# Attention masks on another engine: a select on GpSimd for a minimum on VectorE, and latent sums, root and norm issued one by one

## The reference

```
h    = rmsnorm(x) * (1 + sc1) + sh1            # sc1, sh1, ... from c @ w_ada
proj = h @ w_in                                # q_lat 384, kv_lat 256, k_rope 32, swa q 512, k 128, v 128
q    = rmsnorm(q_lat) @ w_qb                   # 8 heads, 64 + 32 with rope
k, v = rmsnorm(kv_lat) @ w_kvb
y_mla = causal softmax attention, 8 heads, over all keys up to the query
y_swa = sliding window of 128 with ALiBi and sinks: own block of 128 keys and the one before
x = x + g1 * concat(y_mla, y_swa) @ w_o
x = x + g2 * relu(rmsnorm(x)... @ w_up)^2 @ w_down
out = rmsnorm(x)
```

## Time and profile before

| | |
|---|---|
| median of three runs | 945.23 us (944.41 to 946.27) |
| profiled execution, its own time | 945.04 us |
| span of its slowest core | 943.4 us (all cores 939.6 to 943.4) |
| mean granted TensorE clock | 0.955 to 0.961 of full speed |
| busy: PE, ACT, DVE, POOL | 829.5, 507.5, 412.7, 172.0 us |

### The profile page before, as it was taken

The page is one execution under the profiler, slowest core; times in us unless marked ns, Lnnn a source line. Parts: engine busy times, 40 slices in busy tenths (PEclk is TensorE's granted clock), DMA queues, the critical chain, the costliest instruction groups (busy, mean ns, idle before and its releaser), DMA issues.

```text
span 943.4 us, 13041 instructions; the slowest of 8 cores (939.6 to 943.4 us)
## 1 busy us (share of the span) xinstructions
PE 829.5 (88%) x4263; PEld 376.0 (40%) x4263; DVE 412.7 (44%) x673; ACT 507.5 (54%) x750; POOL 172.0 (18%) x182
## 2 busy tenths in 40 slices
PE   1758759877988899997998999999999999999994
PEld 0324323433443344443443444444444444444441
DVE  2264778757564752447843122221112222111566
ACT  3056465667776788884886433234443223445543
POOL 6040211212112110345640000000000000003331
PEclk9969979989999899998999999999999999999997
DMA  8993322432320052207838005040143100000224
GB/s 187 167 155 101 101 46 57 101 79 46 56 46 1 1 134 46 90 1 217 141 49 130 1 1 90 11 79 1 22 67 59 32 1 1 1 1 1 90 90 179
DMA packets 13585, 63.11 MB, mean 67 GB/s; under 512 B 1728, under 2 KB 1984, under 8 KB 9808
## 3 DMA queue, kind: packets, MB, share of 16 engines
q0 software_dynamic: 8192, 36.02, 23.5%
q1 hardware_dynamic: 5328, 26.27, 8.2%
HBM read 89.90 MB, written 8.39 MB: 104 GB/s over the span
## 4 chain that ended last, share of the span: by engine, by line
PE 74%; DVE 9%; ACT 6%; DMA 5%; issue 4%; POOL 1%; DVEq 0%; ACTq 0%; SPq 0%; POOLq 0%
PE ps L508 65%; PE ps L1021 5%; PE ps L965 5%; DMA arena<-wada 4%; DVE arena L1009 2%; ACT arena L990 2%; DMA arena<-xt 1%; DVE arena L1055 1%; DVE arena L563 1%; DVE arena L1057 1%; ACT arena L512 1%; DVE arena L1328 1%; ACT arena L1278 1%; ACT arena L514 1%; ACT arena L554 0%
## 5 line engine op out<-in xcount | busy, mean ns | idle before, releaser
L508 PE MATMUL ps<-arena 128*128 128x512 bf16 (+3 forms) x3623 | 742.2, 351 | 89.7 <-DMA arena<-wada 25.2
L508 PEld LDWEIGHTS ps<-arena 128*128 128x128 bf16 x3623 | 319.3, 99 | 474.8 <-issue 146.6
L1310 DVE SCALAR_TENSOR_TENSOR arena<-ps,arena 128x512 f32<-128x512 f32 x128 | 95.8, 750 | 314.5 <-PE ps L508 314.5
L1297 ACT ACTIVATE arena<-ps 128x512 f32<-128x512 f32 x128 | 76.4, 597 | 210.3 <-PE ps L508 209.8
L990 ACT ACTIVATE arena<-ps 128x1024 bf16<-128x1024 f32 x158 | 158.8, 1020 | 53.4 <-PE ps L965 27.5
L659 POOL TENSOR_TENSOR arena<-arena 128x512 f32<-128x512 f32 (+2 forms) x49 | 64.0, 1307 | 188.1 <-ACT arena L1156 186.9
L1021 PE MATMUL ps<-arena 128*128 128x512 bf16 (+1 forms) x320 | 87.9, 357 | 9.3 <-DVE arena L1009 8.7
L965 PE MATMUL ps<-arena 128*128 128x512 bf16 (+1 forms) x320 | 88.0, 358 | 3.6 <-ACT arena L990 2.6
L1298 ACT ACTIVATE arena<-arena 128x512 bf16<-128x512 f32 x128 | 80.9, 632 | 12.2 <-ACT arena L1297 0.6
L1013 POOL TENSOR_TENSOR arena<-arena 128x512 bf16<-128x512 f32 x32 | 41.9, 1311 | 201.1 <-ACT arena L1012 109.3
L1156 ACT ACTIVATE arena<-arena 128x512 bf16<-128x512 f32 x56 | 35.4, 632 | 43.0 <-DVE arena L1310 35.6
(11 more groups left out here) (62 smaller groups left out, 360.9 us busy)
## 6 DMA issues: line engine op xcount, KB each, us to landing
arena<-wada POOLq DMA_DIRECT2D x24, 512.0 KB, 7.4
arena<-xt SPq DMA_DIRECT2D x8, 1024.0 KB, 8.9
arena<-xt SPq DMA_DIRECT2D x4, 2048.0 KB, 13.5
arena<-wup POOLq DMA_DIRECT2D x8, 1024.0 KB, 13.5
arena<-wdn POOLq DMA_DIRECT2D x8, 1024.0 KB, 19.4
out<-arena SPq DMA_DIRECT2D x12, 512.0 KB, 3.1
arena<-win POOLq DMA_DIRECT2D x11, 256.0 KB, 40.5
arena<-wo POOLq DMA_DIRECT2D x1, 2048.0 KB, 21.3
```

Source lines behind the costliest of these rows:

```text
L508: S.op("pe", lambda h: h.matmul(bk(bank, rows, cols), lhsT=lhsT, rhs=rhs, start=start, stop=stop), r=r, w=[bankb[bank]])
L1297: S.op("act", lambda h, b=b, rs=rs: h.activation(out=TMP[rs], in_=bk(b), func=AF.Relu), r=[bankb[b]], w=[bTMP[rs]])
L1310: S.op("dve", lambda h, b=b, fb=fb: h.scalar_tensor_tensor(out=X1T[G][:, fb, :], in0=bk(b), scalar=MODCOL[:, 40 + fb:41 + fb], in1=X1T[G][ ...
```

## The change

The mask becomes `affine_select` on POOL: it needs no table and clears the places outside the triangle. It takes one instruction for each triangle: MLA's unit A has two (128 columns; 256 columns), B one (128), an SWA unit two of 512 columns (one for the first block). KEEP and its load are gone, so the search places the arena anew.

The latents' sums, root and norm become three pieces. For G = 0 they follow one another as before. For the streams of G = 1 to 3 the kv sums come before the fifth latent projection, the root after that projection's third matmul, the norm after the first matmul of `kr`; the q sums come behind the first `kp` pair, their root behind the second, the norm behind the third. In the filler of G = 2 the three rope items move behind the spread.

```diff
@@ a_streams: stat_items
                         mm(st["b"], None, None, ONESB, SQ[lat[m]], j == 0, j == len(ms) - 1, [bONES, bSQ[lat[m]]])
-                        if j == len(ms) - 1:
-                            rstd_rows(st["b"], RR[i], bRR[i], nf)
-                            then()
                     out.append(go)
-                return out
+                return out, [(0.0, lambda: rstd_rows(st["b"], RR[i], bRR[i], nf), None)], [(0.0, then, None)]
...
+            if G == 0:
+                kvstat, qstat = kvstat + kvr + kvn, qstat + qr + qn
+            else:
+
+                lats[4] = lats[4][:3] + kvr + lats[4][3:]
+                kr = kr[:1] + kvn + kr[1:]
+                kp = [kp[0] + qstat, kp[1] + qr, kp[2] + qn, kp[3]]
+                qstat = []
+                lats = lats[:4] + [kvstat, lats[4]]
+                kvstat = []
             return lats, kvstat, kr, rope, qstat, kp, vp, qp
...
@@ prologue
-        S.dma("pool", lambda h: h.dma_start(out=KEEP, in_=keep_d), bKEEP, w=[bKEEP])
...
@@ emit_keep
-                v = PT[p][:, 0:n, 0:c]
-                m = rap(KEEP_E0 + 128, [[256, n], [1, c]])
+                for i in range(n):
+
+                    k = 1 if i == 0 else c // 128
+                    v = PT[p][:, i, 0:128 * k].rearrange("p (a q) -> p a q", a=k, q=128)
+                    select(v, [[0, k], [1, 128]], -1, 0, p)
             else:
-                i0 = 0 if u.n > 0 else 1
-                v = PT[p][:, i0:2, :].rearrange("p a (g q) -> p a g q", g=4, q=128)
-                m = rap(KEEP_E0 + i0 * 128, [[128, 2 - i0], [0, 4], [1, 128]])
-            S.op("dve", lambda h: h.tensor_tensor(out=v, in0=v, in1=m, op=ALU.min), r=[bPT[p], bKEEP], w=[bPT[p]])
+                for i in range(0 if u.n > 0 else 1, 2):
+                    v = PT[p][:, i, :].rearrange("p (g q) -> p g q", g=4, q=128)
+                    if i:
+                        select(v, [[0, 4], [1, 128]], -1, 0, p)
+                    else:
+                        select(v, [[0, 4], [-1, 128]], 1, -1, p)
+
+        def select(v, pattern, cm, base, p):
+            S.op("pool", lambda h: h.affine_select(out=v, in_=v, pattern=pattern, compare_op=ALU.is_ge, fill=0.0, base=base,
+                                                   channel_multiplier=cm), r=[bPT[p]], w=[bPT[p]])
...
@@ filler of G = 2
-                    filler += flat(spread(groups + body, adas(20, 24)) + kp + vp + qp)
+                    filler += flat(spread(groups + body[:-3], adas(20, 24)) + rope + kp + vp + qp)
```

More of the change, by code:

```diff
@@ L277, in build_program @@
     csx_d = din("csx", [128, T])
-    keep_d = din("keep", [128, 640])
     auxk_d = din("auxk", [4, 1024])
@@ L399, in build_program @@
         SWV_E0 = a_SWV.lo // 2
-        a_KEEP, KEEP = region("KEEP", [128, 640], BF16, "sa012x3y")
-        bKEEP = Buf("KEEP", a_KEEP)
         ESK, bESK = tile1("ESK", [128, 512], F32, "sa012x3y")
@@ L777, in a_streams @@
             lats = [it(proj(rot, m, lat_after(m), G)) for m in range(5)]
-            kvstat = it(stat_items([0, 1], 0, 256, kv_norm))
+            kvs, kvr, kvn = stat_items([0, 1], 0, 256, kv_norm)
+            kvstat = it(kvs)
             rope = [[(6.0, rope_add, None)], [(4.0, lambda: rope_copy(0), None)], [(4.0, lambda: rope_copy(4), None)]]
             kr = it(group(rot, None, None, [(winr2(k), HT[:, k, :], [bWINR, bHT[k]]) for k in range(8)], rope_after))
-            qstat = it(stat_items([2, 3, 4], 1, 384, q_norm))
+            qs_, qr, qn = stat_items([2, 3, 4], 1, 384, q_norm)
+            qstat = it(qs_)
             kp = [it(group(rot, None, None, [(WKV[:, c, hp * 128:(hp + 1) * 128], KVN[:, c, :], [bWKV, bKN[c]])
@@ L913, in build_program @@
         ada_dma(9, 1)
-        KEEP_E0 = a_KEEP.lo // 2
         MLA_SCALE = float(96 ** -0.5)
@@ L1365, in _host_consts @@
     csx = np.concatenate([np.ones((64, T)), np.cos(ang), np.sin(ang) * sgn], axis=0).astype(np.float32)
[L1366 to L1371, removed]
     pos = np.arange(1024)
@@ L1384, in _host_consts @@
                 auxq[kv, 3, n, g] = -128.0 * s8 * (1 - n % 2)
-    return csx, keep, auxk, auxq.reshape(8, 2048)
+    return csx, auxk, auxq.reshape(8, 2048)
 def _tiles(w, nblk, bc):
@@ L1414 @@
     wdn_l = f(w_down)[0].reshape(4, 8, 128, 1024).transpose(0, 2, 1, 3).reshape(512, 8192)
-    csx, keep, auxk, auxq = _host_consts()
+    csx, auxk, auxq = _host_consts()
     col = lambda a: f(a).reshape(-1, 128).T
@@ L1420 @@
         "wo": _tiles(wo_l, 1, 1024), "wup": _tiles(f(w_up)[0], 4, 1024), "wdn": np.ascontiguousarray(wdn_l),
-        "csx": csx, "keep": keep, "auxk": auxk, "auxq": auxq,
+        "csx": csx, "auxk": auxk, "auxq": auxq,
     }
```

## The result

The changed kernel takes 982.3 us (median of its four runs; 980.3 us the fastest) where the kernel before takes 945.1: the ratio is 1.0387, 95% interval 1.0368 to 1.0407, 37 us slower. One of the four runs, 1096.9 us, was a disturbed one; the ratio and every time from here on are taken without such runs, which makes the changed kernel's median 981.7 us.

What follows compares the result with a forecast made beforehand. No engine was full; PE lost 64 us of the attention stages in short waits, plus clock. 945.04 less 37 us of gains plus 33 of losses gave 941, rounded to 940 us; own range 933 to 943, 8 in 10 runs 925 to 957.

Steps and rivals of the forecast that it cites:

- masks off DVE: Attention stages: PE's mask waits give 14 us, two thirds of 17 us of other DVE waits give 12.
- slower rival: At S1: select of 1.1 us, no wait given back, losses 48.5 us against gains of 37; 957 us, chance 0.35.
- norm apart: Latents' statistic in pieces: DVE's 3.62 us hold goes, PE's waits for L700 and L512 shrink; gain 6 us, between 0 and 9.5.
- clock: PE's granted clock: fewer long waits in the 0.87 stretch gain 4 us; longer waits elsewhere lose 3, between 0 and 6.
- S1 behind the product: At 11 places in G = 1 to 3, S1's mask waits behind POOL's normalising product: 33 us, of which 26 stand.
- other waits on POOL: In G = 3, masks stand behind the filler's squares and sums: 4 us lost, between 0 and 8.
- waits for MLA masks on POOL: Sign of being wrong: such waits would mean that a queued load or product holds the mask.
- mild places: S1 in G = 1: the mild case shown costs nothing; the four places were taken at a mean of 2.0 us each.
- four fifths: Share of S1's 33 us left, 26, after DVE and ACT catch up; 33 if nothing comes back, 18 if more merges.
- Nothing to see: Rival: DVE's waits turn into waits for ACT, gain and loss shrink to some 15 each; 943.5 to 947 us, chance 0.13.
- MLA masks: MLA selects on POOL called harmless: A needs some 1.3 us there, the product with V comes three units later.
- Selects: On POOL: 0.85 us for 512 columns, between 0.48 and 1.31; 0.6 for 256, 0.5 for 128; 104 us in all.

Runs made afterwards that it cites:

- e11: The kernel before with no masks at all, the window's scores scaled by a fifth, and the statistic in three pieces: 920.7 us, ratio 0.9742.
- e5: The changed kernel with only POOL's order different, the normalising product issued behind the select of its turn: 948.0 us, ratio 1.0009.
- e12: The changed kernel with masks issued first, the product with V four units behind instead of three, and five PT buffers: 942.4 us, ratio 0.9969.
- e2: The kernel before with only the selects on POOL, the statistic together, KEEP still loaded but unread: 986.5 us, ratio 1.0441.
- e6b: The kernel before with no masks at all, statistic together, the window's scores scaled by a fifth: 924.9 us, ratio 0.9775.
- e4: The changed kernel with the latents' statistic issued together as before, KEEP and its load gone: 985.2 us, ratio 1.0430.
- e10: The changed kernel with only the SWA masks on POOL and the MLA masks on DVE: 976.1 us, ratio 1.0329.

## Why the prediction was wrong

By the runs, the sum is 945.1 - 24.5 (masks off DVE and the split, `e11`) + 61 (the selects, the changed kernel less `e11`) = 981.7. The prediction had - 37 and + 33. The mechanism of the slower rival was the right one, its place too ("The mask of S1 now stands behind L1013"); what failed are sizes. With `e5`, in which no select of S1 stands behind the product of its own turn, the 61 us fall in two parts:

| | predicted, us | measured, us |
|---|---|---|
| gains: masks off DVE, norm apart, KEEP, clock | 37 | 24.5 (`e11`) |
| S1 behind the product | 26 | 34 to 36 (changed less `e5`) |
| other waits on POOL, with their clock | 4 + 3 | 25 to 27 (`e5` less `e11`) |

**The step that failed most: "Other waits on POOL", 4 us, between 0 and 8.** With its clock it is mis-sized by 18 to 20 us, nearly half of the miss of 41. `e5` still waits 22.8 us for selects. In the changed kernel the waits at places other than S1's are 19 of the 55.4 us. The prediction saw that masks in G = 3 stand behind the filler's squares and sums and took it for small; it is not. The wait for an MLA mask is shown above; an SWA mask fares no better, here S0's in G = 3 of the changed kernel:

```profile
433.20 1.04 POOL L1171 TENSOR_TENSOR arena<-arena 128x512 bf16<-128x512 f32 x1 [1.87 <-DVE arena L1182]
434.39 1.15 POOL L656 TENSOR_TENSOR arena<-arena 128x512 f32<-128x512 f32 x1
435.49 1.40 POOL L1021 TENSOR_SCALAR_AFFINE_SELECT arena<-arena 128x512 bf16<-128x512 bf16 x2
437.03 1.04 PE L505 MATMUL ps<-arena 128*128 128x512 bf16 x3 [3.43 <-POOL arena L1021]
```

The swap leaves this wait as it is (3.44 us in `e5`). In `e5` four waits in G = 3 behind a square and a sum make 13.4 us (2.96, 3.44, 1.56, 5.45), and one in G = 1, for an MLA mask behind a product of the turn before, 3.42. The prediction had named "waits for MLA masks on POOL" as a sign of being wrong, and in the changed kernel they are 9.1 us. PE's busy time adds to it: 827.4 us in `e5`, 819.6 in `e11`. How the 25 to 27 us divide between the two is open: `e12` has 10.1 us of waits for selects and still stands 21.5 us above `e11`.

**"S1 behind the product", 26 us.** The right mechanism and the largest loss, mis-sized by 8 to 10 us. `e5` prices it: waits and time go together (32.6 us of waits). Three things were wrong in it.

- The mild places. I took PE's start in the trace of before as the time at which it needs the mask, and the earlier trace rows gave no wait at all. But PE started late there because it waited 1.83 us for a mask that itself stood behind the kv norm, which the same change takes out of the way. The sum's matmul had held PE just ahead of it, too, for 1.92 us on L512; in `e2`, where the statistic stays together, the place costs only 1.46 us. In the changed kernel, at that place, PE stood 4.52 us:

```profile
204.46 0.59 PE L505 MATMUL ps<-arena 128*128 128x512 bf16 x2
209.57 1.01 PE L505 MATMUL ps<-arena 128*128 128x512 bf16 x2 [4.52 <-POOL arena L1021]
```

  and POOL's product started at 206.71, after PE was ready (209.57 - 4.52 = 205.05) and not 3.4 us ahead of its start:

```profile
206.71 1.26 POOL L1026 TENSOR_TENSOR arena<-arena 128x512 bf16<-128x512 f32 x1 [7.40 <-ACT arena L1025]
207.93 1.40 POOL L1021 TENSOR_SCALAR_AFFINE_SELECT arena<-arena 128x512 bf16<-128x512 bf16 x2
```

  The four places of G = 1 have 4.95, 4.52, 1.33 and 2.64 us, 13.4 in all; I had taken 8.
- "I let four fifths stand." Nothing came back. The 11 places have 34 us of waits: 13.4 in G = 1, 11.0 in G = 2 (4.86, 3.47, 2.63, and none at the third), 9.8 in G = 3 (4.42, 0.49, 4.92). Two places of G = 0, which was to be covered, have 2.4 more. That is with selects of 0.665 us; with these my own arithmetic gives 33 - 11 x 0.37 = 29, and 23 with four fifths.
- The clock. I had + 3 among the losses and - 4 among the gains. PE's busy time in the stages rose by 9 us, and in `e5` the whole kernel's is 7.4 us lower than in the changed one (827.4 against 834.8).

**Masks off DVE, 14 + 12 and 4 of clock: too large.** `e6b` has 21 us (17 to 25), and that without any mask to wait for. That waits for other DVE lines fall by two thirds was wrong: over the span they are 24.9 us before, 27.2 in `e6b` and 18.1 in the changed kernel, and PE's waits for ACT grow from 29.5 to 36.9 in `e6b`. So part of the relief comes back as waits for ACT, which the rival "Nothing to see" had said; what sets the wait for L534 is not shown.

**Norm apart, 6 us: right in size for the kernel before (8), wrong in its way and in its worth here.** The waits for L512 grew from 3.6 to 7.2 us; the gain came from masks on DVE that no longer stand behind the norm, and with the masks on POOL about 4 us are left of it.

**MLA masks, 0 us.** They cost 5 to 6 us beyond the SWA ones, and 7.5 with masks first. "For an MLA mask this is harmless" was wrong by that much: the duration was harmless (0.83 us a pair), the queue not.

**Selects, 0.85 us for 512 columns.** They take 0.665, inside the bounds of 0.48 and 1.31. The rule from the Trainium skill, GPSIMD Engine Reference, section "Performance pitfalls for Q7 kernels", gave 0.87 or 0.44 us as an estimate; the trace lies between, and the difference of 512 and 128 columns, 0.319 us for 384, is 1.0 cycles a column at that page's 1.2 GHz, so its unrolled figure with some 0.24 us on top. The price at which the slower case was to decide, 1.05 us, was worthless: that case decided at 0.665.

**KEEP and placement, 1 and 0 us.** Right within what can be measured (`e2`, `e4`).

**Shared port, 0.** The mean of POOL's product did not change (1309 ns, before 1311), though single ones took 1.70 and 1.72 us beside a DVE scale of x. Three selects of 128 columns took 1.88 us at 215.23, beside DVE's add of the rope key (L736), and 1.07 at 430.26. The trace so agrees in kind with what the prediction quotes from the Trainium skill, SBUF — State Buffer, section "Who interferes with whom". In sum it is small: DVE is busy 372.1 us with the selects and 372.0 in `e6b` without them.

## What to carry to other kernels

When an operation moves to an engine that looks idle, look at what will stand ahead of it in that engine's queue, and write down for each neighbour what it waits for: here a 0.7 us select inherited a wait of log, exp and product, and a swap in one queue was worth 34 us. Do it for all neighbours and not only for the one that looks worst: the filler's square and sum, taken for small, were in the way as well. The start of a waiting instruction is not the time at which it could start; where the same change takes its wait away, count from when its other inputs are ready. A wait that is a latency can be bought off with one more unit of distance and a buffer; test that before moving work back.

## What the runs showed of the hardware

A select of 128, 256 and 512 columns of bf16 takes 0.346, 0.429 and 0.665 us on POOL in the mean. On 128 columns that is far less than the 0.61 of the one-input operation with a scalar operand; its shape was no guide. Two on one buffer take 1.39 us together, 0.06 more than twice one. Long waits go with a slower PE: in the changed kernel the same 4263 matmuls were busy 5.3 us longer over the span than before (834.8 against 829.5), with the granted clock at 0.91 in G = 3 against 0.96. Over the kernels of the study whose traces have all 4263 records, those with 48 to 57 us of waits for masks or selects (changed, `e4`, `e10`) have PE busy 834.8 to 839.2 us, and those with less than 23 us 819.6 to 830.2.
